# Diagonal-root transposes, late weight sums on VectorE and an earlier up product in a hybrid encoder block

## What is computed

```python
hn = _rmsnorm(h, mix_norm_g)
q, k, v, ca, cg = split(hn @ w_in)
mixed = concat([stick_breaking_attention(q, k, v), silu(layernorm(dwconv(ca * sigmoid(cg))))])
h = h + mixed @ w_out                                    # (1024 x 1024) weights
hn = _rmsnorm(h, ffn_norm_g)                             # h * rsqrt(mean(h*h) + eps) * g
h = h + (silu(hn @ w_gate) * (hn @ w_up)) @ w_down       # d_ff = 2816
out = _rmsnorm(h, final_norm_g)[meta tokens dropped]
```

## Time and profile before

| | us |
|---|---|
| median of 3 runs | 1174.21 (1173.94 to 1174.76) |
| profiled execution, its own time | 1174.17 |
| span from its first to its last instruction | 1172.4 |
| PE busy | 1151.2 (98% of the span) |
| DVE busy | 693.5 (59%) |
| POOL busy | 451.2 (38%) |
| ACT busy | 435.7 (37%) |
| mean granted TensorE clock | 0.998 |

### The profile page before, as it was taken

The page is one execution under the profiler, slowest core; times in us unless marked ns, Lnnn a source line. Parts: engine busy times, 40 slices in busy tenths (PEclk is TensorE's granted clock), DMA queues, the critical chain, the costliest instruction groups (busy, mean ns, idle before and its releaser), DMA issues.

```text
span 1172.4 us, 15242 instructions
## 1 busy us (share of the span) xinstructions
PE 1151.2 (98%) x5890; PEld 986.8 (84%) x5890; DVE 693.5 (59%) x757; ACT 435.7 (37%) x875; POOL 451.2 (38%) x356
## 2 busy tenths in 40 slices
PE   9999999999999999989999999999999999999997
PEld 5899899899999888867888888888888888888886
DVE  5339898888898646694444445353435353534347
ACT  6321553533737644454141413132322222232323
POOL 4116000000000013267474646556564647473822
PEclk9999999999999999999999999999999999999999
DMA  7204312113026011122030202121212121212114
GB/s 265 81 10 100 71 48 72 38 49 85 13 54 227 19 37 54 36 72 62 13 102 5 87 22 73 36 72 36 72 37 72 37 72 36 72 37 72 37 36 162
DMA packets 70911, 75.69 MB, mean 65 GB/s; under 512 B 11513, under 2 KB 60149, under 8 KB 70840
## 3 DMA queue, kind: packets, MB, share of 16 engines
q1 hardware_dynamic: 69656, 72.60, 20.0%
q10 hardware_dynamic: 1184, 2.13, 0.5%
HBM read 64.13 MB, written 6.32 MB: 60 GB/s over the span
## 4 chain that ended last, share of the span: by engine, by line
PE 69%; DVE 5%; POOL 3%; issue 2%; ACT 0%; POOLq 0%; DVEq 0%; ACTq 0%
PE ps L1820 31%; PE ps L1841 20%; PE ps L1771 8%; PE ps L1631 6%; DVE gq L1298 3%; PE ps L1704 2%; POOL wa_lo L639 1%; DVE acc L1213 1%; PE ps L1689 1%; PE ps L1677 1%; POOL wb_lo L639 1%; DVE wo_lo L1236 0%; PE ps L1784 0%; PE ps L1754 0%; PE ps L1747 0%
## 5 line engine op out<-in xcount | busy, mean ns | idle before, releaser
L1486 DVE TENSOR_TENSOR mix<-ps,mix 128x512 f32<-128x512 f32 x176 | 121.7, 691 | 137.4 <-PE ps L1841 137.4
L1213 DVE SCALAR_TENSOR_TENSOR acc<-u_pad,par,acc 128x1024 f32<-128x1024 f32 x116 | 144.4, 1292 | 1.5 <-ACT acc L830 1.4
L1841 PE MATMUL ps<-wd_hi,act_hi 128*128 128x512 f32 x352 | 137.0, 389 | 0.3 <-DVE act_lo L1475 0.3
L1841 PE MATMUL ps<-wd_lo,act_hi 128*128 128x512 f32 x352 | 136.9, 389 | 0.0
L1841 PE MATMUL ps<-wd_hi,act_lo 128*128 128x512 f32 x352 | 136.9, 389 | 0.0
L625 POOL TENSOR_SCALAR ln_var<-bn 128x1 f32<-128x1 f32 x8 | 3.6, 450 | 338.7 <-DVE bn L1335 338.7
L1631 PE MATMUL ps<-hn_hi,wp_hi 128*128 128x348 f32 (+2 forms) x352 | 118.4, 336 | 0.0
L1631 PE MATMUL ps<-hn_lo,wp_hi 128*128 128x348 f32 (+2 forms) x352 | 117.6, 334 | 0.0
L1631 PE MATMUL ps<-hn_hi,wp_lo 128*128 128x348 f32 (+2 forms) x352 | 117.5, 334 | 0.0
L639 POOL TENSOR_TENSOR wa_lo<-raw,wa_hi 128x512 fp32r<-128x512 f32 x44 | 61.8, 1406 | 142.5 <-ACT wa_hi L1002 142.5
L1051 ACT ACTIVATE act_f<-ps 128x512 f32<-128x512 f32 x22 | 13.1, 598 | 246.1 <-PE ps L1820 246.1
(11 more groups left out here) (187 smaller groups left out, 2644.8 us busy)
## 6 DMA issues: line engine op xcount, KB each, us to landing
raw<-in_w_gate SPq DMA_DIRECT2D x11, 1024.0 KB, 5.3
raw<-in_w_up SPq DMA_DIRECT2D x11, 1024.0 KB, 5.3
wd_f<-in_w_down SPq DMA_DIRECT2D x11, 1024.0 KB, 4.8
raw<-in_w_in SPq DMA_DIRECT2D x16, 512.0 KB, 3.8
xin<-in_x SPq DMA_DIRECT2D x8, 512.0 KB, 10.4
wo_raw<-in_w_out SPq DMA_DIRECT2D x4, 1024.0 KB, 9.5
mix<-in_x SPq DMA_DIRECT2D x8, 512.0 KB, 3.4
out<-ost SPq DMA_DIRECT2D x7, 512.0 KB, 2.6
```

Source lines behind the costliest of these rows:

```text
L1213: dve.scalar_tensor_tensor(out=acc[:, j % 2, :], in0=u_pad[:, p % 2, j:j + L], scalar=par[:, p, j:j + 1], in1=acc[:, j % 2, :], op0=ALU.mu ...
L1486: dve.tensor_tensor(hrow, ps[:, TB + n % 4, :], hrow, ALU.add).then_inc(d_added, 1)
L1841: last = pe.matmul(ps[:, TB + n % 4, :], a[s][:, t, i * P:(i + 1) * P], w_[m][:, t, dh * BANK:(dh + 1) * BANK], start=(t == 0 and s == m = ...
```

## The change

- The scaling of the row before the transposes goes (`norm_h` on DVE). POOL multiplies the identity by the root into `h_diag` (128x128, two buffers), and PE multiplies the unscaled row by that diagonal with plain float32 matmuls in place of the transposes.
- The gain is applied on the way out of PSUM: ACT takes the first four 128-column parts, one operation each (`evac_h`), DVE the second four in one operation (`evac_h_high`). It is loaded as `g2c` (a column for each part) and no more spread over all partitions (`g2b`). `hf_ready` becomes `hf_low` and `hf_high`.
- `square_h` no longer waits for the transposes of the tile before.
- On the DVE stream of the loop, `evac_h_high(i - 2)` stands right behind `residual(i - 1)`, ahead of `ln_stats` and `mix_lo(i, 1)`.
- In the first two blocks six weight sums and seven low parts move from POOL to DVE (`first_sum`, `first_lo`); POOL waits for `tlo_ready` 5 before it goes on.
- Up projection's second product (1, 2) moves ahead of (0, 3) and (0, 5), and its weights are loaded early together with those of (1, 1). Slots, orders and counts follow. The gate's `silu(0, "C11")`, the copies and the high parts on ACT are put in another order.

```diff
-        FIRST_P = [(0, 1), (0, 2), (1, 1), (0, 3), (0, 5), (1, 2), (0, 6), (1, 5), (0, 7), (1, 6), (0, 4), (1, 7), (1, 3), (1, 4)]
+        FIRST_P = [(0, 1), (0, 2), (1, 1), (1, 2), (0, 3), (0, 5), (0, 6), (1, 5), (0, 7), (1, 6), (0, 4), (1, 7), (1, 3), (1, 4)]
+        LO_DVE = [(0, 3), (0, 4), (0, 5), (0, 6), (1, 5), (0, 7), (1, 6)]
+        SUMS_DVE = [(0, "S2"), (0, "S4"), (0, "S3"), (1, "S1"), (1, "S2"), (1, "S4")]
...
 block.sync
-            sp.dma_start(g2b[:, :], ffn_norm_g[0].partition_broadcast(P)).then_inc(g2_loaded, 16)
+            sp.dma_start(g2c[:, :], ffn_norm_g[0].rearrange("(k p) -> p k", p=P), allow_slow_non_contiguous=True).then_inc(g2_loaded, 16)
...
-            sp.dma_start(w_f_of(NTH[1, 1]), w_up_t[:, 0:KH, 0:P]).then_inc(fu_loaded, 16)
+            for k, ks in ((1, slice(0, KH)), (2, slice(KH, KD))):
+                sp.dma_start(w_f_of(NTH[1, k]), w_up_t[:, ks, 0:P]).then_inc(fu_loaded, 16)
...
 block.gpsimd
+                pool.wait_ge(h_rstd, i + 1)
+                if i >= 2:
+                    pool.wait_ge(ht_ready, i - 1)
+                pool.tensor_scalar(h_diag[:, i % 2, :], ident[:, :], rstd[:, n:n + 1], None, ALU.mult).then_inc(h_diag_ready, 1)
...
+                if i == TILES - 1:
+                    pool.wait_ge(ms_used, TILES)
+                    weight_sum(0, 5)
...
             h_root(TILES - 1)
-            weight_sum(0, 3)
-            weight_lo(0, 3)
-            weight_lo(0, 5)
-            weight_lo(0, 4)
-            weight_lo(0, 6)
-            weight_lo(1, 2)
-            weight_sum(1, 5)
-            weight_sum(1, 6)
-            weight_lo(1, 5)
+            pool.wait_ge(tlo_ready, 5)
             weight_sum(1, 7)
-            weight_sum(1, 3)
-            weight_lo(1, 6)
             weight_lo(1, 7)
+            weight_lo(1, 4)
             weight_lo(1, 3)
-            weight_lo(1, 4)
...
 block.scalar
-                act.activation(hn2f[:, i // 4, :, c],
-                               ps[:, TB:TB + 2, :].rearrange("p b (k t) -> p (b k) t", k=4), ACT.Copy).then_inc(hf_ready, 1)
+                for k in range(KH):
+                    act.activation(hn2f[:, i // 4, k, c], ps[:, TB, k * P:(k + 1) * P], ACT.Identity,
+                                   scale=g2c[:, k:k + 1], bias=zeros[:, 0:1]).then_inc(hf_low, 1)
...
+            evac_h(TILES - 1)
+            hi_h(TILES - 1)
             weight_hi(0, 6)
             weight_hi(0, 3)
-            evac_h(TILES - 1)
-            hi_h(TILES - 1)
+            t_high("T1", 6, 8)
             weight_hi(0, 4)
-            t_high("T1", 6, 8)
             copy(0, 1)
+            weight_hi(0, 7)
+            t_high("T2", 4, 6)
             t_high("T2", 6, 8)
...
 block.vector
+                dve.tensor_tensor(hn2f[:, i // 4, KH:KD, c], ps[:, TB + 1, :].rearrange("p (k t) -> p k t", k=KH),
+                                  g2c[:, KH:KD].unsqueeze(2).to_broadcast([P, KH, P]), ALU.mult).then_inc(hf_high, 1)
...
                     residual(i - 1)
+                if i >= 2:
+                    evac_h_high(i - 2)
                 if i + 1 < TILES:
                     ln_stats(i + 1)
                 mix_lo(i, 1)
...
-                if i >= 1:
-                    norm_h(i - 1)
...
             residual(TILES - 1)
+            evac_h_high(TILES - 2)
+            t_low(1, "T1", 4, 6)
             for t in ("T2", "T4"):
                 t_sum(t, 5)
-            t_low(1, "T1", 4, 6)
-            norm_h(TILES - 1)
             t_sum("T1", 6)
             lo_h(TILES - 2)
+            t_sum("T3", 6)
+            first_sum(0, 6)
+            first_sum(0, 3)
+            evac_h_high(TILES - 1)
+            first_sum(0, 7)
+            lo_h(TILES - 1)
             t_sum("T1", 7)
-            lo_h(TILES - 1)
-            t_sum("T3", 6)
-            t_low(3, "T1", 6, 8)
+            first_lo(0, 3)
+            t_low(2, "T1", 6, 8)
+            first_lo(0, 4)
+            first_lo(0, 5)
             t_sum("T3", 7)
             for i in (6, 7):
                 t_sum("T2", i)
+            first_lo(0, 6)
             t_low(3, "T2", 4, 6)
             t_low(4, "T2", 6, 8)
+            first_sum(1, 5)
+            first_sum(1, 6)
             for i in (6, 7):
                 t_sum("T4", i)
+            first_lo(1, 5)
+            first_lo(0, 7)
+            addition(0, "U4")
+            first_sum(1, 3)
+            t_low(5, "T3", 4, 8)
+            first_lo(1, 6)
+            t_low(6, "T4", 4, 8)
             addition(0, "C11")
-            t_low(5, "T3", 4, 8)
-            addition(0, "U4")
-            t_low(6, "T4", 4, 8)
             addition(1, "C11")
...
 block.tensor
-                    last = pe.transpose(ps[:, TB + k // 4, (k % 4) * P:(k % 4 + 1) * P],
-                                        xn2[:, k * P:(k + 1) * P], ident[:, :])
+                    last = pe.matmul(ps[:, TB + k // 4, (k % 4) * P:(k % 4 + 1) * P],
+                                     hrow[:, k * P:(k + 1) * P], h_diag[:, i % 2, :], start=True, stop=True)
```

More of the change, by code:

```diff
@@ L193, in hybrid_block @@
         bn6 = keep("bn6", [P, 6], F32)
+        g2c = keep("g2c", [P, KD], F32)
         bn2 = keep("bn2", [P, 2 * TILES], F32)
@@ L341, in hybrid_block @@
         LO_NTH = {p_: n for n, p_ in enumerate(LO_ORDER)}
-        SLOT = FIRST_SLOT + [(0, 5, 1, 2, 4, 3)[n % SLOTS] for n in range(len(LATER))]
+        SLOT = FIRST_SLOT + [(0, 4, 1, 2, 5, 3)[n % SLOTS] for n in range(len(LATER))]
         def slot_freed(n):
@@ L349, in hybrid_block @@
         COPIES = [(0, 1), (0, 5), (1, 1), (1, 5)] + [(b, k) for b in range(2, BLOCKS) for k in (1, 5)]
-        ADDITIONS = ([(0, "C11"), (0, "U4"), (1, "C11"), (0, "C22"), (0, "C12"), (1, "U4"), (1, "C22"), (1, "C12")]
+        ADDITIONS = ([(0, "U4"), (0, "C11"), (1, "C11"), (0, "C22"), (0, "C12"), (1, "U4"), (1, "C22"), (1, "C12")]
                      + [(b, c_) for b in range(2, BLOCKS) for c_ in ("U4", "C11", "C22", "C12")])
@@ L371, in hybrid_block, with low_done @@
         SUM_OF = {5: "S1", 6: "S2", 3: "S4", 7: "S3"}
+        SUMS_POOL = [(0, "S1"), (1, "S3")] + [(b, s_) for b in range(2, BLOCKS) for s_ in ("S1", "S2", "S4", "S3")]
+        SUMS_DVE = [(0, "S2"), (0, "S4"), (0, "S3"), (1, "S1"), (1, "S2"), (1, "S4")]
         def summed(b, s_):
-            order = {0: ("S3", "S1", "S2", "S4"), 1: ("S1", "S2", "S3", "S4")}.get(b, ("S1", "S2", "S4", "S3"))
-            return 4 * b + order.index(s_) + 1
+            if (b, s_) in SUMS_DVE:
+                return s_summed_dve, SUMS_DVE.index((b, s_)) + 1
+            return s_summed, SUMS_POOL.index((b, s_)) + 1
+        def low_done(b, k):
+            if (b, k) in LO_DVE:
+                return flo_dve, LO_DVE.index((b, k)) + 1
+            return flo_done, LO_NTH[b, k] + 1
         QUARTERS = {"C11": (0, 0), "C12": (0, 1), "C22": (1, 1), "C21": (1, 0)}
@@ L393, in hybrid_block @@
         T_SUMS = ([(t, i) for i in (4, 5) for t in ("T1", "T3", "T2", "T4")]
-                  + [(t, i) for t in ("T1", "T3", "T2", "T4") for i in (6, 7)])
+                  + [(t, i) for i in (6, 7) for t in ("T1", "T3")] + [(t, i) for t in ("T2", "T4") for i in (6, 7)])
         def t_cols(i0, i1):
@@ L1032, in _ @@
                     act.wait_ge(ms_used, TILES)
+                    weight_hi(0, 5)
                     t_high("T1", 4, 6)
@@ L1096, in _ @@
                     copy(b, k)
+                if (b, k) == (0, 7):
+                    silu(0, "C11")
                 while weights < min(n + SLOTS - 1, len(PRODUCTS)):
@@ L1349, in residual, with evac_h_high @@
                     dve.tensor_tensor(hrow[:, c], ps[:, (PJ, PV)[i % 2] + dh, :], hrow[:, c], ALU.add).then_inc(h_ready, 1)
-            def norm_h(i):
+            def evac_h_high(i):
                 if i == 0:
                     dve.wait_ge(g2_loaded, 16)
-                dve.wait_ge(h_rstd, i + 1)
-                n = TILES + 1 + i
-                dve.scalar_tensor_tensor(out=xn2[:, :], in0=mix[:, i, :, :].rearrange("p k t -> p (k t)"),
-                                         scalar=rstd[:, n:n + 1], in1=g2b[:, :], op0=ALU.mult, op1=ALU.mult).then_inc(hn_ready, 1)
+                dve.wait_ge(ht_ready, i + 1)
+                c = slice((i % 4) * P, (i % 4 + 1) * P)
+                dve.tensor_tensor(hn2f[:, i // 4, KH:KD, c], ps[:, TB + 1, :].rearrange("p (k t) -> p k t", k=KH),
+                                  g2c[:, KH:KD].unsqueeze(2).to_broadcast([P, KH, P]), ALU.mult).then_inc(hf_high, 1)
             def lo_h(i):
@@ L1864, in _ @@
             product(1, 1)
+            pe.wait_ge(h_ready, 2 * TILES)
+            product(1, 2)
             pe.wait_ge(hlo_ready, TILES)
@@ L1869, in _ @@
             product(0, 5)
-            pe.wait_ge(h_ready, 2 * TILES)
-            product(1, 2)
             pe.wait_ge(tlo_ready, 4)
             product(0, 6)
-            pe.wait_ge(hf_ready, TILES)
+            pe.wait_ge(hf_low, KH * TILES)
+            pe.wait_ge(hf_high, TILES)
             product(1, 5)
```

92 lines of the change are left out of this document (57 added, 35 removed).

## The result

The changed kernel takes **1177.44 us** (median of 8 runs, 1176.98 to 1178.11) against 1174.08 of the kernel before in the same comparison (8 runs). The ratio is 1.003 with a 95% interval of 1.0019 to 1.0041: 2.2 to 4.8 us slower. The forecast was 1176.7. The profiled execution of the changed kernel is one of 1177.03 us, with a span of 1175.2.

A forecast was written before the change was run, and what follows sets the result against it. PE was taken to bound the kernel. +4.6 us for the products ahead of T and -2.1 behind it gave +2.5 on 1174.21, forecast 1176.7 us, range for 8 in 10 1172.4 to 1179.6.

The forecast's parts named there:

- The product's price: In the loop of tiles diagonal products take PE 1.79 us a tile, 0.92 more than transposes: +4.6 us ahead of T.
- T: Start of tile 5's transposes on PE (487.29 us in the kernel before), from which the forecast counts its later times.
- third rival: On PE, the diagonal product costs no more than a transpose: 1169.3 us; chance 5%.
- The queue ahead of `w_out_part(7, 1)`: On DVE evac_h_high(5) delays mix_lo(7, 1): PE starts at T + 3.33, idle 1.5 us instead of 0.7.
- The waits that go: PE's waits ahead of tile 7's products (1.4 us), (0, 3) (2.0) and (2, 6) (0.7) vanish, low clock too.
- the rival of the falling clock: PE's clock falls again behind new waits in the stretch behind T, price 1.6 us: 1178.3 us; chance 15%.
- The three stalls of VectorE: PE waits on late DVE ahead of (0, 6), 1.1 us, (1, 5), 0.8, and (0, 7), 1.3.
- The rival that VectorE is not late: DVE has T2's low part for tokens 6 and 7 by T + 29.0 instead of 30.05: 1172.9 us; chance 16%.
- The rival of a late load: Up load lands after 8 us instead of 5.5, delaying (1, 5), (0, 7), (0, 4) by 2.5: 1179.2; chance 10%.
- The stall ahead of (0, 4): PE waits 0.5 us ahead of product (0, 4), until T + 43.65, for DVE's additions and product beside POOL's work.
- The stretch behind T: T to the start of product (2, 6) on PE takes 60.0 us against 62.1 before, -2.1 us.
- The sum at (2, 6): Up to product (2, 6) on PE: +4.6 ahead of T and -2.1 behind it, +2.5 us.

The follow-up runs named there:

- Experiment 1: The changed kernel with its eight float32 products per tile put back into transposes, the root left out: 1170.82 us.
- experiment 2: The kernel before with its eight transposes per tile issued as plain float32 products against the identity: 1179.48 us.
- experiment 3: The changed kernel with mix_lo(7, 1) ahead of evac_h_high(5) on VectorE in the last iteration: 1176.05 us.
- experiment 6: The changed kernel with product (1, 2) back behind (0, 3) and (0, 5), its weights still loaded early: 1178.71 us.
- Experiments 4 and 5: The changed kernel with addition(0, C22) ahead of the product behind silu: 1177.34 us; the changed kernel without GpSimd's wait for tlo_ready 5: 1176.78 us.
- experiments 8 to 10: Onto the kernel with ScalarE scaling: addition(0, C22) earlier, silu(0, C11) later, pause tlo_ready 4, 1168.22 us; plus sum (1, 7) on VectorE, 1168.74; or instead pause 5, 1168.78.
- experiments 7 to 10: The changed kernel with ScalarE scaling the row, then transposes, and mix_lo(7, 1) ahead of evac_h_high(5): 1169.84 us; the others are experiments 8 to 10.

## Why the prediction was right, and which term was off

**The product's price: right.** 128 records for 64 products, 1.78 us a tile (forecast 1.79), tiles 13.63 us apart (13.67), and T 4.35 us later (4.6), of which 0.2 is where the loop began. Experiment 1 takes it off and experiment 2 puts it on the kernel before, with all else the same (in experiment 1 the root is left out). The third rival, that a diagonal product costs no more than a transpose, falls.

**The queue ahead of `w_out_part(7, 1)`: right.** Forecast start T + 3.33, measured 494.97 - 491.64 = 3.33; experiment 3 takes the wait out alone.

**The waits that go: right.** Neither tile 7's products nor (0, 3) nor (2, 6) is waited for, and the clock stays at 1.00, so the rival of the falling clock did not come to pass. The reason given against it was weak: the two waits behind which it fell before lay 5.7 us apart, while those ahead of (0, 6), (1, 5) and (0, 7) lie 3.8 us apart and it did not fall. It stayed at 1.00 with transposes too (experiment 1), so the products are not needed for it. Without (1, 2) moved up, (0, 3) waits again (experiment 6).

**How waits are to be compared.** A 128x512 matmul's row is 0.39 us long where its step is 0.227. The idle time in a row is therefore 0.16 us shorter than the delay from step to step, in which the forecast was made. By steps the five delays are 1.54, 0.95, 0.93, 0.96 and 1.71 us.

**The three stalls of VectorE: right in place, order and about in size.** Forecast 1.1, 0.8, 1.3; measured 0.95, 0.93, 0.96. The starts behind them are T + 29.77 for 30.1, 33.56 for 33.6 and 37.36 for 37.7. The rival that VectorE is not late falls: it wanted (0, 6)'s low parts by T + 29.0. The rival of a late load falls too: it was issued at T + 24.5 (forecast 24.75) and took 5.4 us (5.5):

```profile
516.10 0.38 SPq L529 DMA_DIRECT2D raw<-in_w_up  x1
```

**The stall ahead of (0, 4): mis-sized.** Forecast 0.5, measured 1.71 by steps (1.55 in the row). The failing step is "ACT's high part (1, 7) waits for that sum until 39.4": from its start at 37.7 I gave GpSimd's sum 1.7 us. It started at T + 37.4, but beside VectorE's subtractions, which follow each other without a gap, it took 3.87, and ACT waited until T + 41.35. Experiments 4 and 5 show this place from both sides: the stall goes when the addition no longer stands behind that queue, and when the sum is made earlier.

**The stretch behind T.** It came out at 61.1 us for 60.0, and this one stall is the difference. (1, 6) still started 0.2 us ahead of the forecast, at T + 40.2 for 40.45; (0, 4) started 1.0 late, at T + 44.65 for 43.65, and from there to (2, 6) it is 16.4 us, for 16.35. That the idle times in the rows sum to 5.3 us, for 5.2 forecast, is a coincidence of two ways of counting: by steps they are 6.1, and the restarts behind them cost some more. The sum at (2, 6) is +3.3 for +2.5: 1.1 from this stall, less 0.25 ahead of T.

**The rest of the difference.** The profiled spans are 2.8 us apart and the medians 3.4; the forecast was 2.5, and the interval is 2.2 to 4.8. From profile to profile the work ahead of the loop shifts by some tenths up to 1.4 us (`w_out_part(7, 1)` starts at 489.21, 488.89 and 490.34 in experiments 8 to 10, which do not differ there), so what is below about half a microsecond in the times is not settled here. Behind T the traces are steadier: (0, 6) starts at T + 26.26 to T + 26.29 in experiments 7 to 10.

## What to carry to other kernels

Count records, not calls: a float32 matmul of 128 columns on PE is two records here where a float32 transpose is one. Folding a scaling into a transpose by means of a diagonal therefore doubles its price, and where PE is the bound that is paid in full. When the bound is one engine, give the scaling to an engine with room, here ScalarE, and check each operation that you put into a queue for what stands behind it in the last iteration, where the loop's cover is gone. When a wait is mended and the time stays, look for a second way by which the same late operation reaches the bound.

## What the runs showed of the hardware beyond that

- GpSimd's 128x512 sum took 3.87 us when VectorE's subtraction over 2048 columns of two operands ran beside it, 1.80 beside one of 512 columns, and 1.29 with VectorE idle. The Trainium skill, "SBUF — State Buffer", section "SBUF: two separate sides", says that the port pair which the two engines share is locked for the whole of an instruction, also by a VectorE operation with two inputs in SBUF against a GpSimd one that reads it. The traces agree: VectorE's sum became 1.57 from 0.69 beside GpSimd's, and GpSimd's long one, begun at 529.03, ended 1.14 us after VectorE's subtraction did (531.76), about its time alone. It had begun during a short subtraction of VectorE (528.86 to 529.54) and was held through the long one behind it as well, so back-to-back operations held it for more than one of them.
- The product of diagonal and identity on GpSimd (128x128, one operand and a scalar) took 0.61 us for six of the eight tiles, where I had taken 0.4, and 0.91 and 1.71 for the other two (at 484.18 and 503.64); it had cover in every tile.
- PE waited 2.3 us ahead of one product in experiment 2 (and 0.9 us some 5 us earlier), and its granted clock stayed at 1.00 there; in the kernel before it fell behind waits of 1.2 and 1.8 us that lay 5.7 us apart. Which of it decides was not tried.
